# Gating stage of a decoder layer: elementwise chains shifted by one step, norm squares and transposes issued a tile earlier, sums of squares by a selector product

## The reference

```
h    = rmsnorm(x, pre_mix_g)
u, v, gate, xr = split(h @ w_in)                 # four parts of 2048 columns
y_a  = gelu(u) * (tril(w_spatial) @ rmsnorm_per_head(gelu(v)) + b_spatial)   # in chunks of 128 positions
y_b  = rglru(conv4(xr)) * gelu(gate)             # a recurrence over the positions
y    = [rmsnorm(y_a), rmsnorm(y_b)] @ w_out
x    = x + rmsnorm(y, post_mix_g)
x    = x + rmsnorm(swiglu(rmsnorm(x, pre_ffn_g)), post_ffn_g)
```

## Time and profile before

| | us |
|---|---|
| median of the runs | 5605.98 |
| profiled execution, its own time | 5615.9 |
| its span on the slowest core (core 7) | 5614.3 |
| spans of the eight cores | 5593.1 to 5614.3 |
| start of the first `v` products (step 0) | 55.2 |
| start of the first `u` products (step 8) | 208.4 |
| start of the recurrent stage (step 0) | 678.3 |
| start of its step 1 | 713.6 |
| start of the output product | 1402.9 |
| TensorE busy over the span | 5296.8 (94%) |
| VectorE, ScalarE busy over the span | 1164.0 (21%), 1203.5 (21%) |

### The profile page before, as it was taken

One profiled execution on the slowest core, in us unless ns is written; L12 is line 12 of the kernel. 1 busy time (PEld: TensorE's weight loads), 2 busy tenths in 40 slices (PEclk: granted clock), 3 DMA queues, 4 the chain that ended last, 5 costly groups with the idle time before them and its releaser, 6 DMA issues.

```text
span 5614.3 us, 63138 instructions; the slowest of 8 cores (5593.1 to 5614.3 us)
## 1 busy us (share of the span) xinstructions
PE 5296.8 (94%) x24992; PEld 2416.4 (43%) x24992; DVE 1164.0 (21%) x1785; ACT 1203.5 (21%) x1856; POOL 280.7 (5%) x444
## 2 busy tenths in 40 slices
PE   3789899999899579999999999999999999999998
PEld 1344344444344234444444444444444444444443
DVE  3443346655212330000000000000110000011006
ACT  3554357777222330000011000000000000000003
POOL 0000000000000000000000000000000000000005
PEclk8899999999999789999999999999999999999998
DMA  6686423223755864443466443336774433377759
GB/s 168 131 156 153 79 59 67 54 52 76 172 109 126 237 170 77 79 78 74 82 125 136 97 79 76 75 70 133 168 173 79 77 75 75 69 165 165 152 127 319
DMA packets 178041, 650.83 MB, mean 116 GB/s; under 512 B 48978, under 2 KB 49362, under 8 KB 134866
## 3 DMA queue, kind: packets, MB, share of 16 engines
q0 software_dynamic: 54144, 372.27, 38.1%
q1 hardware_dynamic: 123604, 274.51, 15.1%
HBM read 903.87 MB, written 115.08 MB: 181 GB/s over the span
## 4 chain that ended last, share of the span: by engine, by line
PE 87%; DMA 6%; DVE 2%; ACT 2%; issue 2%; SPq 0%; DVEq 0%; ACTq 0%; POOL 0%; POOLq 0%
PE ps L413 56%; PE ps L1127 20%; PE ps L838 7%; PE ps L526 2%; DMA SB<-x_own 2%; DMA out<-SB 2%; DVE SB L300 2%; DMA hscr<-SB 1%; DMA yscr<-SB 1%; ACT SB L297 1%; ACT SB L455 0%; PE ps L437 0%; ACT L297 0%; SPq L294 0%; DMA SB<-oscr 0%
## 5 line engine op out<-in xcount | busy, mean ns | idle before, releaser
L413 PE MATMUL ps<-SB 128*128 128x512 bf16 x15104 | 3295.9, 381 | 32.6 <-DMA SB<-hscr 27.7
L413 PEld LDWEIGHTS ps<-SB 128*128 128x128 bf16 x15104 | 1478.4, 98 | 1815.0 <-issue 66.4
L1127 PE MATMUL ps<-SB 128*128 128x512 bf16 x5504 | 1210.9, 384 | 0.0
L297 ACT ACTIVATE SB<-ps 128x512 f32<-128x512 f32 (+1 forms) x476 | 315.2, 665 | 3437.5 <-PE ps L413 2980.5
L1127 PEld LDWEIGHTS ps<-SB 128*128 128x128 bf16 x5504 | 543.8, 99 | 666.5 <-issue 73.2
L303 DVE TENSOR_TENSOR SB<-SB,ps 128x512 bf16<-128x512 f32 x172 | 118.3, 688 | 2591.4 <-PE ps L413 2582.7
L300 DVE SCALAR_TENSOR_TENSOR SB<-SB 128x512 f32<-128x512 f32 (+2 forms) x520 | 462.2, 901 | 361.5 <-ACT SB L297 241.3
L838 PE MATMUL ps<-SB 128*128 128x512 bf16 x2048 | 453.3, 385 | 0.0
L297 ACT ACTIVATE SB<-SB 128x512 f32<-128x512 f32 (+2 forms) x448 | 307.0, 705 | 179.7 <-DVE SB L300 143.0
L838 PEld LDWEIGHTS ps<-SB 128*128 128x128 bf16 x2048 | 202.7, 99 | 248.4 <-issue 26.1
L526 PE MATMUL ps<-SB 128*128 128x512 bf16 x1024 | 242.7, 399 | 63.2 <-DVE SB L445 56.7
(11 more groups left out here) (59 smaller groups left out, 745.7 us busy)
## 6 DMA issues: line engine op xcount, KB each, us to landing
SB<-w_fi POOLq DMA_DIRECT2D x172, 1024.0 KB, 8.1
SB<-w_fm POOLq DMA_DIRECT2D x48, 1024.0 KB, 13.1
fscr<-SB SPq DMA_DIRECT2D x192, 256.0 KB, 6.4
SB<-w_fo POOLq DMA_DIRECT2D x48, 896.0 KB, 9.1
SB<-w_fo POOLq DMA_DIRECT2D x48, 768.0 KB, 7.7
SB<-w_o POOLq DMA_DIRECT2D x32, 1024.0 KB, 8.9
out<-SB SPq DMA_DIRECT2D x64, 512.0 KB, 10.4
SB<-fscr SPq DMA_DIRECT2D x128, 256.0 KB, 10.2
```

The lines of the kernel that those rows point to most:

```text
L297: S.op("act", lambda e: e.activation(out=out, in_=in_, func=func, **kw), r=r, w=w)
L413: ins = e.matmul(PS[bank][:, :].rearrange("p (t n) -> p t n", n=128), lhsT=v[:, kc, :], rhs=ht[:, 4 * half:4 * half + 4, kc, :], start=(kc ...
L1127: ins = e.matmul(PS[bank][:, :], lhsT=abs_[k].ap[:, tg * 128:(tg + 1) * 128], rhs=v[:, k, :], start=(first and k == 0), stop=(last and k = ...
```

## The change

The diff, cut to the parts that the prediction speaks of:

```diff
-    def xload(src, tg, buf, halves=2):
+    def xload(src, tg, buf):
+        for q in range(4):
+            t = A(XT[buf].r[1] + q * 4096, 1024)
+            dma_in(t, src[tg * 128:(tg + 1) * 128, q * 1024:(q + 1) * 1024], ("xt", buf, q))
...
+    cload(IDF.ap, ident_d, IDF.r, "idf")
     xload(x_own, 0, 0)
-    cload(TRI.ap, tri_d, TRI.r)
-    cload(IDF.ap, ident_d, IDF.r)
-    cload(pv.ap, pv_d, pv.r)
-    cload(flag.ap[:, 0:1], flag_d, flag.r)
     for q in range(4):
         t_ = A(GAIN.r[1] + q * 4096, 1024)
         dma_in(t_, gpre_d[:, q * 1024:(q + 1) * 1024], ("gain", q))
+    dma_in(GVB, gv_d[:, 0:512], "gvb")
     xload(x_own, 1, 1)
+    cload(TRI.ap, tri_d, TRI.r)
...
-    dma_in(GVB, gv_d[:, 0:512], "gvb")
+    cload(pv.ap, pv_d, pv.r, "pv")
+    cload(flag.ap[:, 0:1], flag_d, flag.r, "flag")
...
-    def ssq_mm(ysq, colbase, half):
-                ins = e.matmul(SSQ[:, c:c + 1], lhsT=ysq.ap[:, t * 128:(t + 1) * 128], rhs=ONEC.ap[:, 0:1],
+    def ssq_mm(ysq, row, first=False, last=False):
+        S.op("pe", lambda e: e.matmul(SSQ[0:4, :], lhsT=SEL.ap[:, row * 4:row * 4 + 4], rhs=ysq.ap, start=first, stop=last),
...
-        def own_elem(t):
+        def own_sq(t):
             for q in range(4):
                 sq_piece(t % 2, q, t % 2)
             sq_rstd(t % 2)
+
+        def own_xn(t):
             for q in range(4):
                 xn_piece(t % 2, q, t % 2, XN4[q])
-            if t + 2 < 8:
-                xload(x_own, t + 2, t % 2)
+                if t + 2 < 8:
+                    xpiece(x_own, t + 2, t % 2, q)
...
         def own_tps(t):
-                pcopy("act" if q % 2 == 0 else "dve", d.ap, d.r, 3 + q)
+                pcopy("act" if q == 0 else "dve", d.ap, d.r, 3 + q)
         def prev_xn(idx):
-            if q == 0:
-                sq_rstd(i % 2)
...
-            if q == 3 and i + 2 < 8:
-                xload(x_prev, i + 2, i % 2)
+            if i + 2 < 8:
+                xpiece(x_prev, i + 2, i % 2, q)
         def prev_sq(idx):
+            if q == 3:
+                sq_rstd(i % 2)
...
         def mix_elem(hd, half, gu):
-            k = k_[0] % 2
+            k = k_[0] % 3
...
-        own_elem(0)
-        own_tps(0)
-        v_units(0)
+        xq = A(XT[0].r[1] + 12288, 1024)
+        units["v"] = [ring_load(w_v[i], r=[xq.r] if i == 0 else ()) for i in range(4)]
+        own_sq(0)
+        own_xn(0)
+        own_tps(0)
+        own_sq(1)
+        own_xn(1)
         for s in range(64):
+            if s < 7:
+                own_tps(s + 1)
+            if 11 <= s < 43:
+                prev_tp(s - 11)
...
-            for m in mixes:
-                mix_mm(m[0], m[1])
             for q in sqs:
                 ssq_mm(*q)
-            if s < 7:
-                own_elem(s + 1)
-            if s == 0:
-                setup_mix()
             for m in mixes:
                 mix_elem(*m)
+            if s > 0:
+                elem(s - 1)
+            for m in pend_mix:
+                mix_mm(m[0], m[1])
+            if s == 0:
+                own_sq(2)
+            if s < 6:
+                own_xn(s + 2)
             if 10 <= s < 42:
                 prev_xn(s - 10)
-            if r < 8:
-                v_elem(hg, r)
...
-            if 11 <= s < 43:
-                prev_tp(s - 11)
+            if s < 5:
+                own_sq(s + 3)
             if 6 <= s < 38:
                 prev_sq(s - 6)
-            if s < 7:
-                own_tps(s + 1)
-            if s == 44:
-                for t in range(7):
+            if s == 2:
+                setup_mix()
+            if s == 50:
+                for t in range(8):
                     d = A(R1 + t * 8192, 4096, BF16)
                     dma_in(d, hscr[t], ("htp", t), [("hscr", t)])
...
-                        if i == 0 and tg == 0:
+                        if i == 0 and tg == 1:
                             pe1(63)
                             a2(63)
                             d2(63)
                             a3(62)
                             a3(63)
-                            ssq_mm(YSQ[0], 31, 0)
                         if i == 1 and tg == 3:
-                            ssq_mm(YSQ[1], 31, 1)
+                            ssq_mm(YSQ[0], 2)
+                        if i == 1 and tg == 4:
+                            ssq_mm(YSQ[1], 3, last=True)
+                            S.op("dve", lambda e: e.tensor_copy(out=SSX.ap[0:4, :], in_=SSQ[0:4, :]), r=[("ps", 7)], w=[SSX.r])
+                        if i == 1 and tg == 6:
+                            S.op("pe", ssx_t, r=[SSX.r, ID4.r], w=[("ps", 7)])
...
+                            for t2 in range(7):
                                 ev_a(t2, TMPA[t2], t2)
```

More of the change, by code:

```diff
@@ L237, in build_program @@
     ident = ps_.take(128, BF16)
-    ones = ps_.take(128, BF16)
+    bias = ps_.take(128, BF16)
     pv = ps_.take(NV)
@@ L279, in ring_load @@
         t = A(RING + s * UNIT, m * 512, BF16)
-        S.op("pool", lambda e: e.dma_start(out=t.ap, in_=src_ap), w=[t.r], dma=("ring", s))
+        S.op("pool", lambda e: e.dma_start(out=t.ap, in_=src_ap), r=list(r), w=[t.r], dma=("ring", s))
         return t
@@ L313, in build_program @@
     T7 = Bump(R1 + 57344, R1 + 65536)
-    YST_G = [T7.take(512, BF16) for _ in range(2)]
-    YSQ_G = [T7.take(512, BF16) for _ in range(2)]
+    YST_G = [T7.take(512, BF16) for _ in range(3)]
+    YSQ_G = T7.take(512, BF16)
     GU = [T7.take(512) for _ in range(2)]
@@ L324, in build_program @@
     wsT = gm.take(2048, BF16)
-    bias = gm.take(2048, BF16)
+    SELB = gm.take(2048, BF16)
     VN = [gm.take(512, BF16) for _ in range(8)]
@@ L362, in build_program @@
     S.op("dve", lambda e: e.tensor_copy(out=ident.ap, in_=IDF.ap), r=[IDF.r], w=[ident.r])
+    S.op("dve", lambda e: e.memset(SELB.ap, 0.0), w=[SELB.r])
+    S.op("dve", lambda e: e.memset(bias.ap, 0.0), w=[bias.r])
+    for p in (0, 32):
+        S.op("dve", lambda e, p=p: e.tensor_copy(
+            out=SELB.ap[p:p + 16, :].rearrange("p (h n) -> p h n", n=128),
+            in_=IDF.ap[p:p + 16, p:p + 16].unsqueeze(2).to_broadcast([16, 16, 128])), r=[IDF.r], w=[SELB.r])
+    S.op("dve", lambda e: e.tensor_copy(out=ID4.ap, in_=IDF.ap[:, 0:4]), r=[IDF.r], w=[ID4.r])
     def setup_mix():
@@ L639, in build_program @@
     XCB = [rm.take(512, BF16) for _ in range(2)]
-    YSQ = [rm.take(512, BF16) for _ in range(2)]
-    YST = [rm.take(512, BF16) for _ in range(2)]
     TR = rm.take(512)
@@ L644, in build_program @@
     A2 = rm.take(512)
+    YSQ = [rm.take(512, BF16) for _ in range(2)]
+    YST = [rm.take(512, BF16) for _ in range(2)]
     def rglru(carry):
-        pend_mix, pend_ssq, mix_mm, mix_elem = carry
+        to_elem, pend_mix, pend_ssq, mix_mm, mix_elem, g_elem = carry
         NSTEP = 64
@@ L767, in rglru @@
             pe0(k)
-            if k == 0:
+            if k < 3:
+                sqs = list(pend_ssq)
+                pend_ssq.clear()
+                mixes = list(to_elem)
+                to_elem.clear()
+                for q in sqs:
+                    ssq_mm(*q)
+                for m in mixes:
+                    mix_elem(*m)
+                if k == 0:
+                    g_elem(63)
                 for m in pend_mix:
                     mix_mm(m[0], m[1])
-                for q in pend_ssq:
-                    ssq_mm(*q)
-                pend_ssq.clear()
-                for m in pend_mix:
-                    mix_elem(*m)
-                t7 = A(R1 + 7 * 8192, 4096, BF16)
-                dma_in(t7, hscr[7], ("htp", 7), [("hscr", 7)])
-            if k == 1:
-                for q in pend_ssq:
-                    ssq_mm(*q)
+                to_elem.extend(pend_mix)
+                pend_mix.clear()
             a1(k)
```

130 lines of the change are left out of this document (66 added, 64 removed).

## The result

The changed kernel takes 5681.17 to 5716.35 us, the kernel before 5599.6 to 5605.98 on the same chip: a ratio of 1.0171, 95% interval 1.0119 to 1.0222, so 1.7% **slower**. The forecast was 5560, 0.8% faster, with a range of 5510 to 5606; the time lies outside it. (Executions in which the cores of a die ran disturbed are left out of all ratios here.) The profiled execution took 5681.17 with a span of 5679.5 us, 65 more than the 5614.3 of before.

The account below looks back on a forecast made before the run. It took TensorE's products as the bound, with waits before 1448 us as all the change could touch. Terms -33 + 35 + 3 + 0 - 13.4 - 30.5 - 14 + 7 = -46 gave 5560 us by the median, range 5510 to 5606.

Parts of the forecast that it names:

- u steps: Steps with x_prev whose chain lacks sum and gain: its 7.2 us loop is covered by 7.9 of TensorE work, no loss.
- v steps: Steps 17 to 24 and a group later: x_prev's transposes wait for its scaling, loss 35 us and 3 for slower products.
- Opening: Steps 0 to 7: overlapped work makes a step 14.5 us, first u products at 175.5 instead of 208.4, gain 33.
- Stores: Stores of x_prev: two staging buffers remain, waits taken at 0; bounds 20 us gained and 45 lost.
- Step 48: Loads moved from step 44 to 50: the 11.77 us wait and 1.6 of slow products go, gain 13.4.
- recurrent stage: Its step 1: tile 7's load, now issued at step 50, no longer holds products, gain 30.5 us.
- Output product: First block: the 11.07 us wait goes and 1.5 of 3.26 stay; gain 14 us, bounds 10 and 15.
- Sums of squares: One 512-column product replaces four one-column products: 0.11 us more for each of 64, loss 7.
- the covered wait: Rival: x_prev's transposes find their input each step, terms of 35 and 3 go, gain 84, 5522 us; chance 0.26.
- the opening without gain: Rival: opening steps wait for their tiles, step 8 starts at 208 again; gain 13, 5593 us; chance 0.16.
- the quarters: Rival: x_prev's quarter loads in SyncE's queue delay stores, five waits add 55 us, 5615; chance 0.12.

Follow-up runs that it names:

- e1: The changed kernel with two buffers for the gating chain's squares again and two for its stores: 5569.3 to 5598.7 us, ratio 0.9956 to the kernel before.
- e2: The changed kernel, one square buffer kept, with the sum of squares ahead of its step's products on TensorE: 5561.6 to 5587.7 us, ratio 0.9958.
- e5: The kernel before with one buffer instead of two for the gating chain's squares, nothing shifted: 5592.0 to 5626.4 us, ratio 1.0002.
- e9: e6 with the opening's squares and scalings laid into the gaps of the chain: 5501.6 to 5540.5 us, ratio 0.9856.
- e10: e9 with step 0's products ahead of tile 1's transposes: 5500.6, 5501.6 and 5504.9 us, ratio 0.9823.
- e3: e1 with the transposes of x_prev last in the step, behind the products: 5550.9 to 5575.6 us, ratio 0.9918.
- e8: e4 with the recurrent stage's loads where they stood before (seven at step 44, tile 7 behind the last store): 5578.6 and 5582.7 us.
- e11: e6 with the output product's first block ordered as in the kernel before: 5520.0, 5521.1 and 5545.1 us, ratio 0.987.
- e4: e3 with each sum of squares again four one-column products instead of one 512-column selector product: 5533.3 to 5541.4 us, a fourth execution 5579, ratio 0.9898.
- e7: e4 with x_prev loaded in halves instead of quarters: 5521.1 and 5532.6 us, ratio 0.9858.
- e6: e4 with the first four weight loads issued at once, not held for tile 0: 5511.97 to 5513.99 us, ratio 0.9833.

## Why the prediction was wrong

**The step that failed** is the wait that the forecast put at nothing in the u steps: "In u steps the chain has no sum and gain (7.2, with 1.3 for mix_elem in it) against 7.9: covered." It added up the ring from the transposes on and took the chain to start as soon as ScalarE's copy is done. But ahead of the chain on ScalarE stands the square, and that waits for its buffer. The premise behind it is a sentence on the sums of squares: "The three store buffers free a wait that no row of TensorE shows: nothing." It priced what was given to the stores and never asked where the memory came from. It came from the squares, two buffers to one; their reader is TensorE's L430, behind the products; and that put the ring above through every u step. What stood in place of nothing is 40 us in steps 8 to 17 alone, and 114 from step 8 to step 66 against e1. e1 and e2 each take the ring away by another means and gain some 120 us, e5 shows that it needs the shift. The rule that was used for the v steps (add up one turn of the ring, not the load of an engine) would have found it: 0.5 from L430 to the square, 0.5 to the chain, 2.8 up to the scaling, 1.3 for the scaling and 0.25 to the transposes make 5.3, on top of the products.

With that ring out, the sum was near: 5560 against 5569 to 5599 in e1. By its terms:

- **Opening**, -33: -33.5 in the profiled execution (174.94 against 208.4). Right, also in that the order of the work on VectorE and ScalarE set the step, as e9 shows, and not step 0's start, on which the forecast spent its longest working (e10).
- **v steps**, +35 and 3: e1 has 81.1 and 80.5 where the kernel before has 62.3 and 61.6, +38. 79.7 was forecast for each. Right.
- **Stores**, 0: the value hid two effects. In e1 steps 25 to 33 gained 5 to 9; with the transposes last, in e3, that is lost again. That slow v steps give the queue time, as the forecast had it, fits both but has no run of its own.
- **Step 48**, -13.4, and **recurrent stage**, -30.5: e8 measures 44 for the two. Right.
- **Output product**, -14: -7 in the changed kernel, 7 to 8 by e11. Half. The sum of squares found its tile, but the last gate's bank was the next to be late; it wasn't asked for.
- **Sums of squares**, +7: e4 measures 17 to 20, and 0.31 us for each of 32 in the recurrent stage, which is 20 for 64. The earlier trace rows priced the old form well; the new one was priced as a product of 512 columns, at 0.22. It is followed after 0.31, and the product ahead of it, too, gives way 0.31 later instead of 0.22:

```profile
1001.69 0.38 PE L738 MATMUL ps<-SB 128*128 128x512 bf16 x1
1002.00 0.38 PE L430 MATMUL ps<-SB 128*4 128x512 bf16 x1
1002.31 7.08 PE L421 MATMUL ps<-SB 128*128 128x512 bf16 x32
```

As measured, these terms add up to about -32, not -46 (-33.5 + 38 - 5 - 44 - 7.5 + 20), so 5574 from the median of before. That e1 lies so near the forecast is in part the stores' gain, which was not forecast.

Of the rivals, the covered wait and the opening without gain fell by the rows above, and the quarters by e7. The slower side was given 0.02 over 2% and 0.12 in all, on a mechanism that wasn't there, while the one that was stood in the diff.

The ring of the square buffer is shown by runs, and so are the terms of the v steps, of step 48 and the recurrent stage, of the output product and of the sums of squares. Two things are open. Steps 41 to 49 take 64.7 to 77.0 us on the cores of one execution of e6. The traces put it down to the stores: on the core with 66.8 ScalarE waits 16.0 us for them and TensorE 4.5 for VectorE, on the one with 77.0 it is 25.1 and 12.2. Why the stores land later on one core than on another is not known. And in the last stretch, behind the output product's first block, the changed kernel's core was 18 us quicker than the core of before. That one stood at a granted clock of 0.87 and 0.81 in the two stretches of 50 us from 5450 on, which is 16. All eight cores of the kernel before show it there and none of the changed one, and why is not known.

## What to carry to other kernels

When buffers change hands in a diff, list for each one that shrinks who writes it, who reads it last, and what stands ahead of that reader on its engine; add up one turn of the ring that this closes. The single buffer was harmless here with its reader ahead of the long work of the step (e2), and in the order of before, where nothing behind it was due earlier (e5). The cheapest cure was to move a 0.4 us instruction, not to find memory. An early start on an engine is worth nothing if a later step has a later input of its own: ask for the last arrival, not the first.

## What the runs showed of the hardware

**The granted clock falls to 0.81 on pairs of cores, for a stretch of 80 to 160 us, in the midst of dense products.** In one execution of e4, first core 1, then core 5:

```profile
180.00:200.00 20.00, 20.00 (x80) 8.42 (x79) 7.71 (x14) 12.63 (x19) 0.53 (x1) 0.81 1.03 170
220.00:240.00 20.00, 20.00 (x103) 9.31 (x102) 6.76 (x10) 11.49 (x17) 0.53 (x1) 0.81 0.79 152
2100.00:2200.00 100.00, 100.00 (x465) 45.38 (x464) 4.81 (x7) 4.19 (x7) 3.69 (x7) 1.00 0.40 74
```

```profile
220.00:240.00 20.00, 20.00 (x131) 10.35 (x130) 7.34 (x11) 14.08 (x21) 1.05 (x2) 1.00 0.90 173
```

From 220 to 240 us TensorE is busy 20.00 of 20 us on both cores, and does 103 products on the one and 131 on the other. 0.81 is neither of the two levels, 1.2 and 2.4 GHz, between which the clock goes after a stop. In seven of the thirteen profiled executions such a stretch begins at 146 to 163 us, as the opening's gaps end on all cores at once; others begin at 309 to 504 us, near 1945 and from 5414 on, and four executions have none. By its length times one minus the clock a stretch is worth 16 to 30 us, as much as the terms disputed here, and only the slowest core counts. The Trainium skill (TensorE: Matmul & The Clock Gate, section Seeing it yourself) knows this level, 13/16, as a limit on current that takes a whole die once three of its cores run dense matmuls, and lasts while they do. The level agrees with the rows; the rest doesn't: here two cores of a die have it and the other two not, and later, with all eight dense, it is gone, as in the third row. Why it takes these cores wasn't found; stages must be compared on cores without it, and medians of runs say less than the step starts of one core.

**A product behind a selector of four columns costs more than a full one**: 0.31 and 0.1 more for the one ahead, against 0.22 (rows above); four products of one column cost 0.10 together. e4 measures 0.31 for each exchange of the one for the other.
